# Attention over rows of a 2048-token layer: rotary heads in steps of two query tiles, and the order of TensorE's work in a step

## The reference, cut to what matters

```python
SEQ, CHUNK, HEAD_DIM = 2048, 64, 64
# group A: 8 query heads over 2 key heads, rotary, own chunk + 1 before (A_BAND = 2), a sink per head
sc = einsum('bncvgd,bnlvd->bnvgcl', qc, kb) * HEAD_DIM ** -0.5
m  = max(max(sc, axis=-1), sink);  p = exp(sc - m)
p  = p / (sum(p, axis=-1) + exp(sink - m))
oa = einsum('bnvgcl,bnlvd->bncvgd', p, vb)
# group B: 8 heads, own chunk + 8 before (B_BAND = 9), a clipped relative bias per head
sc = einsum('bnchd,bnlhd->bnhcl', qc, kb) * HEAD_DIM ** -0.5 + bias
ob = einsum('bnhcl,bnlhd->bnchd', softmax(sc), vb)
x  = x + concatenate([rmsnorm(oa), rmsnorm(ob)]) @ w_out
```

## Time and profile before

| what | us |
|---|---|
| median of 3 runs (2800.03 to 2801.11) | 2800.1 |
| the profiled execution, its own time | 2800.31 |
| its span from first to last instruction | 2798.5 |
| attention, from the first scores to the last output | 534.46 to 892.48 |

### The profile page before, as it was taken

One profiled execution on the slowest core, in us unless ns is written; L12 is line 12 of the kernel. 1 busy time (PEld: TensorE's weight loads), 2 busy tenths in 40 slices (PEclk: granted clock), 3 DMA queues, 4 the chain that ended last, 5 costly groups with the idle time before them and its releaser, 6 DMA issues.

```text
span 2798.5 us, 41169 instructions
## 1 busy us (share of the span) xinstructions
PE 2741.3 (98%) x14774; PEld 2249.8 (80%) x14774; DVE 1555.9 (56%) x2465; ACT 1091.2 (39%) x2229; POOL 1087.0 (39%) x882
## 2 busy tenths in 40 slices
PE   9999999999999999999998999999999999999998
PEld 9888888777766788888886888887888887888876
DVE  3356664567676332333336666668766666654364
ACT  6434333377787223333325333334333332222342
POOL 7644454301011112311216555455655453552252
PEclk9999999999999999999999999999999999999999
DMA  8657868534366334022326333335333236544454
GB/s 280 235 179 254 267 210 272 172 125 140 115 184 216 135 132 173 32 89 80 91 64 225 113 98 102 98 99 199 120 110 98 90 110 213 219 145 148 139 171 136
DMA packets 260112, 425.45 MB, mean 152 GB/s; under 512 B 18256, under 2 KB 157520, under 8 KB 258896
## 3 DMA queue, kind: packets, MB, share of 16 engines
q1 hardware_dynamic: 222512, 355.29, 38.5%
q10 hardware_dynamic: 37408, 67.65, 7.8%
HBM read 282.35 MB, written 135.27 MB: 149 GB/s over the span
## 4 chain that ended last, share of the span: by engine, by line
PE 55%; DVE 2%; DMA 1%; POOL 1%; ACT 1%; issue 0%; SPq 0%; POOLq 0%; ACTq 0%; DVEq 0%
PE gu_acc L51 10%; PE gu_acc L52 10%; PE gu_acc L53 10%; PE down_acc L51 4%; PE down_acc L53 4%; PE down_acc L52 4%; PE cross_sum_o L51 2%; PE cross_sum_s L51 2%; PE cross_sum_s L53 2%; PE cross_sum_o L53 2%; PE cross_sum_o L52 2%; PE cross_sum_s L52 2%; PE cross_turned L2185 0%; PE cross_turned L1903 0%; DMA gu_t<-t_d 0%
## 5 line engine op out<-in xcount | busy, mean ns | idle before, releaser
L51 PE MATMUL gu_acc<-gu_t,shared_m 128*128 128x512 f32 x704 | 276.0, 392 | 5.0 <-DVE gu_t L2507 5.0
L52 PE MATMUL gu_acc<-gu_t,shared_m 128*128 128x512 f32 x704 | 275.0, 391 | 0.0
L53 PE MATMUL gu_acc<-gu_t,shared_m 128*128 128x512 f32 x704 | 274.9, 391 | 0.0
L350 POOL TENSOR_TENSOR front_wq_lo<-front_wq_raw,front_wq_hi 128x1024 fp32r<-128x1024 f32 x72 | 178.9, 2486 | 201.9 <-ACT front_wq_hi L346 201.7
L2450 ACT ACTIVATE shared_m<-kept_x 128x512 fp32r<-128x512 f32 x175 | 109.4, 628 | 210.8 <-PE gu_acc L53 187.8
L51 PEld LDWEIGHTS gu_acc<-gu_t,shared_m 128*128 128x128 f32 x704 | 132.8, 189 | 35.6 <-issue 4.7
L53 PEld LDWEIGHTS gu_acc<-gu_t,shared_m 128*128 128x128 f32 x704 | 132.7, 189 | 27.8
L52 PEld LDWEIGHTS gu_acc<-gu_t,shared_m 128*128 128x128 f32 x704 | 132.9, 189 | 27.3
L346 ACT ACTIVATE front_wq_hi<-front_wq_raw 128x1024 fp32r<-128x1024 f32 x72 | 76.2, 1058 | 187.0 <-PE qkv_acc L53 100.7
L51 PE MATMUL gu_acc<-shared_m 128*128 128x512 f32 x352 | 138.0, 392 | 2.9 <-POOL shared_m L2423 2.5
L53 PE MATMUL gu_acc<-shared_m 128*128 128x512 f32 x352 | 137.6, 391 | 0.0
(11 more groups left out here) (353 smaller groups left out, 7653.1 us busy)
## 6 DMA issues: line engine op xcount, KB each, us to landing
front_wq_raw<-in_w_in ACTq DMA_DIRECT2D x69, 512.0 KB, 4.0
head_h<-qk_d SPq DMA_DIRECT2D x48, 512.0 KB, 4.6
ahead_w_even<-in_w_gate SPq DMA_DIRECT2D x44, 512.0 KB, 4.5
kept_x<-in_w_up SPq DMA_DIRECT2D x44, 512.0 KB, 4.3
a_d<-gu_a_mix SPq DMA_DIRECT2D x88, 256.0 KB, 3.2
a_d<-gu_a SPq DMA_DIRECT2D x66, 256.0 KB, 4.2
kept_x<-in_w_down SPq DMA_DIRECT2D x56, 256.0 KB, 4.7
shared_m<-a_d SPq DMA_DIRECT2D x19, 704.0 KB, 4.2
```

The costliest lines, as they stand in the source:

```text
L51: pe.matmul(out, l_hi, r_hi, start=first, stop=False)
L52: pe.matmul(out, l_hi, r_lo, start=False, stop=False)
L53: return pe.matmul(out, l_lo, r_hi, start=False, stop=last)
L350: pool.tensor_tensor(self.lo[:, i % Q_SLOTS, :], self.raw[:, i % Q_SLOTS, :], raw(self.hi[:, i % Q_SLOTS, :]), ALU.subtract).then_inc(self ...
```

## The change

The unit u becomes a step s. In group B a step is one unit, as before; in group A it is two query tiles of a job, so A has 32 steps instead of 64. Scores, exponentials, transposes, values, copies and division of a step of A cover both tiles; the two score tiles stand in the two banks of `sum_s`. TensorE's order in a step is now: scores of t, all transposes of t-2, the output's transpose of t-4, values of t-3. The transposes use three banks: in B head 0's first four tiles, head 1's first four tiles, and the fifth tile of both heads with the output's transpose in the same bank; in A one bank for each of the two query tiles. ScalarE copies the first piece, VectorE the rest; VectorE does the score sums of its step first, then copies, then the division of t-4. Nothing in the SyncE block changes: the quarters, the wait at L1274 and `load` are as they were, and `s_o` still counts two for each unit.

```diff
-    UNITS_ALL = [(J, i) for J in range(len(JOBS)) for i in range(NT)]
-    NB = len(UNITS_ALL)
+    STEPS = ([(J, (i,)) for J in range(N_PAIR) for i in range(NT)]
+             + [(J, (i, i + 1)) for J in range(N_PAIR, 2 * N_PAIR) for i in range(0, NT, 2)])
+    NS = len(STEPS)
...
+    def units(s):
+        return s if s <= A0 else A0 + 2 * (s - A0)
+
+    def job_end(J):
+        return NT * (J + 1) if J < N_PAIR else A0 + NT // 2 * (J + 1 - N_PAIR)
...
+    def pieces(s):
+
+        if is_a(s):
+            return [(j, [(j, x, y) for x in range(2) for y in range(tiles(s, j))]) for j in range(2)]
+        near, last = min(tiles(s, 0), 4), [(0, x, 4) for x in range(2) if tiles(s, 0) > 4]
+        return [(j, part) for j, part in ((0, [(0, 0, y) for y in range(near)]),
+                                          (1, [(0, 1, y) for y in range(near)]), (2, last)) if part]
...
-        turned = [room.bank(f"turned{j}") for j in range(2)]
+        turned = [room.bank(f"turned{j}") for j in range(3)]
         sum_o = room.bank("sum_o")
-        o_turned = room.bank("o_turned")
+        o_turned = turned[2][:, 2 * P:4 * P]
...
-                    act.wait_ge(s_out, NB - (1 - z) * HT)
+                    act.wait_ge(s_out, NS - (1 - z) * HT // 2)
...
-                for step in range(NB + 4):
+                for step in range(NS + 4):
                     if step >= 4:
                         copy_o(step - 4)
-                    if 2 <= step < NB + 2:
-                        copy(act, copied, step - 2, 0, 0)
-                    if 1 <= step < NB + 1:
-                        exp(step - 1, 0)
-                    if 2 <= step < NB + 2:
-                        copy(act, copied, step - 2, 1, 0)
-                    if 1 <= step < NB + 1:
-                        exp(step - 1, 1)
-                    J, late = divmod(step, NT)
-                    if late == 7 and 1 <= J < 2 * N_PAIR:
-                        store(J - 1)
-                    if step == NB - HT + 6:
+                    for lane in range(4):
+                        if 1 <= step < NS + 1 and lane < len(lanes(step - 1)):
+                            exp(step - 1, *lanes(step - 1)[lane])
+                        if 2 <= step < NS + 2 and lane == 0:
+                            copy(act, copied, step - 2, *pieces(step - 2)[0])
+                    for J in range(2 * N_PAIR - 1):
+                        if step == job_end(J) + 5:
+                            store(J)
+                    if step == NS + 1:
                         store_last(0)
...
-                for step in range(NB + 5):
-                    if step >= 5:
-                        divide(step - 5)
-                    if 2 <= step < NB + 2:
-                        copy(dve, dve.tensor_copy, step - 2, 0, 1)
-                    if step < NB:
-                        maxima(step, 0)
-                        maxima(step, 1)
-                    if 2 <= step < NB + 2:
-                        copy(dve, dve.tensor_copy, step - 2, 1, 1)
+                for step in range(NS + 4):
+                    if step < NS:
+                        for lane in lanes(step):
+                            maxima(step, *lane)
+                    if 2 <= step < NS + 2:
+                        for j, part in pieces(step - 2)[1:]:
+                            copy(dve, dve.tensor_copy, step - 2, j, part)
+                    if step >= 4:
+                        divide(step - 4)
...
+                    after(pe, s_max, 2 * units(s))
+                    for j, i in enumerate(tokens):
+                        w, end = width(s, j), (i + 1) * P
+                        halves = [(0, w, j * BANK)] if w <= BANK else [(0, w // 2, 0), (w // 2, w, BANK)]
...
+                    for b, part in pieces(s):
+                        j, x, _ = part[-1]
+                        pe.wait_ge(s_exp, 2 * (units(s) + j) + x + 1)
+                        after(pe, s_copied[b], fillings(s, b))
+                        if b == 2:
+                            after(pe, s_out, s - 2)
+                        for z, (j, x, y) in enumerate(part):
+                            at = columns(s, j, tiles(s, j) * P).start + y * P
+                            last = pe.transpose(turned[b][:, z * P:(z + 1) * P], probs(s, x, slice(at, at + P)),
+                                                ident[:, :])
+                        last.then_inc(s_t[b], 1)
...
+                def turn_out(s):
+                    pe.wait_ge(s_o_sb, s + 1)
+                    after(pe, s_out, s)
+                    after(pe, s_copied[2], fillings(s + 2, 2))
+                    for j in range(len(STEPS[s][1])):
+                        last = pe.transpose(o_turned[:, j * P:(j + 1) * P], o_sb[:, s % 2, j * P:(j + 1) * P],
+                                            ident[:, :])
+                    last.then_inc(s_ot, 1)
+
+                for step in range(NS + 4):
+                    if step < NS:
                         score(step)
-                    if 2 <= step < NB + 2:
-                        turn(step - 2, 1)
+                    if 2 <= step < NS + 2:
+                        turn(step - 2)
                     if step >= 4:
                         turn_out(step - 4)
-                    if 3 <= step < NB + 3:
+                    if 3 <= step < NS + 3:
                         values(step - 3)
```

More of the change, by code:

```diff
@@ L1121, in stage_attention, with is_a, lanes, win @@
     A_FULL = A_WIN * P
[L1123 to L1155, removed]
+    def is_a(s):
+        return s >= A0
+    def units(s):
+        return s if s <= A0 else A0 + 2 * (s - A0)
+    def job_end(J):
+        return NT * (J + 1) if J < N_PAIR else A0 + NT // 2 * (J + 1 - N_PAIR)
+    def lanes(s):
+        return [(j, x) for j in range(len(STEPS[s][1])) for x in range(2)]
+    def win(s):
+        return A_WIN if is_a(s) else B_WIN
+    def tiles(s, j):
+        return min(STEPS[s][1][j] + 1, win(s))
+    def width(s, j):
+        return tiles(s, j) * P - (CHUNK if is_a(s) and tiles(s, j) == win(s) else 0)
+    def columns(s, j, w):
+        full = win(s) * P
+        return slice(j * A_FULL + full - w, j * A_FULL + full)
+    def quarter(s):
+        J, tokens = STEPS[s]
+        return J * N_BLK + tokens[0] // BT
+    def pieces(s):
[4 more added lines that the diff above has]
+                                          (1, [(0, 1, y) for y in range(near)]), (2, last)) if part]
+    uses = [[0] for _ in range(3)]
+    for s in range(NS):
+        for j in range(3):
+            uses[j].append(uses[j][-1] + sum(k == j for k, _ in pieces(s)))
+    def fillings(s, j):
+        return uses[j][min(max(s, 0), NS)]
     LOADS = 4
@@ L1210, in stage_attention, with probs, copy @@
         s_wlo = room.sem("s_w_lo")
[L1212 to L1222, removed]
+        def probs(s, x, at):
+            return (probs_a if is_a(s) else probs_b)[:, s % 2, x, at]
+        def copy(engine, instruction, s, j, part):
+            after(engine, s_o, 2 * units(s - 1) if s >= 1 else 0)
+            engine.wait_ge(s_t[j], fillings(s, j) + 1)
+            if j == 2:
+                after(engine, s_ot, s - 1)
+            heads, n = sorted({x for _, x, _ in part}), len(part) * P
+            unit, _, y = part[0]
+            w = n // len(heads)
+            at = unit * A_FULL + y * P
+            instruction(turned_sb[:, s % 2, heads[0]:heads[-1] + 1, at:at + w],
+                        turned[j][:, 0:n].rearrange("p (h c) -> p h c", h=len(heads))).then_inc(s_copied[j], 1)
         def stored(engine):
@@ L1326, in _, with exp @@
             def _(act):
[L1327 to L1332, removed]
-                        act.wait_ge(s_zero, 4)
[L1334 to L1341, removed]
+                def exp(s, j, x):
+                    act.wait_ge(s_max, 2 * (units(s) + j) + x + 1)
+                    for b in range(3):
+                        after(act, s_t[b], fillings(s - 1, b))
+                    if s in (A0, A0 + 1):
+                        act.wait_ge(s_zero, 4)
+                    after(act, s_out, s - 3)
+                    at, lane = columns(s, j, width(s, j)), 2 * j + x
+                    act.activation(probs(s, x, at), scores[:, s % 2, x, at], ACT.Exp,
+                                   bias=top[:, s % 4, lane:lane + 1], scale=-1.0,
+                                   accum_out=total[:, s % 4, lane:lane + 1]).then_inc(s_exp, 1)
+                    if is_a(s) and lane == 3:
+                        act.wait_ge(s_below, s - A0 + 1)
+                        act.activation(sink_exp[:, s % 4, :], below[:, s % 4, :], ACT.Exp).then_inc(s_sink_exp, 1)
@@ L1415, in maxima @@
                         out=to, in0=from_, in1=add, scale=-0.125, scalar=start, op0=ALU.add, op1=ALU.min,
[L1416 to L1424, removed]
-                    else:
[L1426 to L1429, removed]
+                        accum_out=top[:, s % 4, lane:lane + 1]).then_inc(s_max, 1)
@@ L1462, in score @@
```

(32 more changed lines are left out.)

161 lines of the change are left out of this document (76 added, 85 removed).

## The result

The changed kernel takes 2852.5 us (median of 4 runs, 2848.43 to 2855.41) against 2800.15: ratio 1.0185, 95% interval 1.0168 to 1.0203. The profiled execution took 2853.14 us with a span of 2851.4, 52.9 longer than before.

The account below looks back on a forecast made before the run. TensorE, busy 98% of the span, was taken to bound the kernel. Attention's end at 942.8 instead of 892.5 (+50.3) and the border's +3.7 made +54.0 on 2800.3: 2854 us, range 2822 to 2872.

Parts of the forecast that it names:

- Group B: TensorE's new order in group B: one array-shape change fewer a step, full step 3.67 us, -13 us in all.
- The shape rival: TensorE's 0.17 us gaps belong to semaphore waits, not array-shape changes, so group B gains nothing: 2867 us, chance 0.08.
- The bound of -17 us: Largest gain allowed for group B, if the new order brings no new wait; the other bound was 0.
- Steps of two tiles: Group A's pair step costs TensorE 3.10 us against 3.88, ScalarE and VectorE just hidden; by itself 24 us gained.
- One step in front of a load instead of five: Group A's load release: lead before a quarter's scores falls from 9.7 to 3.1 us, so 14 loads come late.
- the 4.5 and 13 that were named as signs: Expected in group A's profile: 14 TensorE DMA waits of 2 to 4.5 us, loads' first DMAs 10.5 to 13 apart.
- The load: A quarter's load in group A takes 7.5 us from first issue to landing, plus 0.1 to the scores.
- The step that closes the loop: Group A's pair step between a load's landing and the next load's issue: 4.9 us, mostly at half clock.
- Behind the last wait: From the scores of step 94 to attention's last output: 6.2, 1.0 for the clock, 2.2 and 6.1, together 15.5 us.
- The border: Attention to next stage: the norm waits for the last job's store, starting 3.2 us after the last output; +3.7 us.
- with the clock up: Rival: group A's loads come late but TensorE's clock holds at 1.00, steps at 3.25 us: 2832 us, chance 0.22.
- with the loads in time: Rival: group A's loads arrive in time and the change gains, 32 us less: 2768 us, chance 0.10.

Follow-up runs that it names:

- run 1: Changed kernel, but group A's queries and keys load once the score sums allow it, values on their own semaphore; 2764.5 us, ratio 0.9869.
- run 3: Changed kernel with 28 filler transposes of the identity on TensorE ahead of each late load's wait in group A; 2827.3 us, ratio 1.0098.
- run 8: Changed kernel, same load release, but keys and values shared by two group A jobs loaded only for the first; 2806.7 us, ratio 1.0026.
- run 5: Kernel before the change, with group A's loads from the third on released two units later; 2877.3 us, ratio 1.0275.
- run 6: Kernel before the change, late group A loads released two units later, 14 filler transposes of the identity ahead of each wait; 2822.1 us, ratio 1.0077.

## Why the prediction was right

The forecast was 2854 us, the measurement 2852.5. By its own steps:

- *Group B*, -13 us: load 18 went out 13.6 us sooner after attention's start, and the full step is 3.67, as summed. The shape rival is out: the transposes wait for three pieces without a gap. The bound of -17 us was added up wrongly; 10.9 and 5 make 16.
- *Steps of two tiles*, 3.10 us with ScalarE and VectorE hidden: 3.11 in run 1.
- *One step in front of a load instead of five*: 14 waits, as counted, and run 1 shows that they are the cause. They last 3.5 to 4.8 us, with loads 11.4 to 13.8 apart, a little past the 4.5 and 13 that were named as signs.
- *The load*, 7.5 + 0.1 us: measured 7.10 from issue to scores, too long by 0.5. The medians of the earlier trace rows held loads that met the old kernel's stores and the next load; with loads 12.5 us apart the values' DMA lands 5.1 us after its issue in the median, where I had 5.7 on average.
- *The step that closes the loop*, 4.9 us: measured 5.47 from scores to the next load, between 4.6 and 5.9, too short by 0.6. The low clock covered most of these steps whole, and such a step takes 5.9 us, not the 5.6 estimated from the values alone.
- *Behind the last wait*, 15.5 us: measured 17.2 (924.79 to 942.00), too short by 1.7. Its last term, 6.1, was rounded up; its parts add up to 5.9.
- *The border*, +3.7 us: the norm begins 3.35 us behind the last output and began 0.55 before it, 3.9.

So the hit to 2 us is partly luck. Two errors of opposite sign, some 7 us each over 13 quarters, leave 12.51 us a quarter where I had 12.5. Two smaller ones cancel in part: load 18 went out 3.0 us sooner than forecast (754.30 against 757.3), 1.9 of it because attention itself began sooner in this execution, and the end took 1.7 longer. The mechanism does not hang on them. Run 1 took away the late load and gave back 88 us, where the forecast and its rival lie 86 apart. The clock's part was 13 x 1.65 + 1 = 22 us in the sum; run 3 gave 25 and left about 5. Run 8 shortened the load in eight quarters and gave 46 where 38 were expected.

Two of the rivals were priced right and are other kernels: with the clock up 2832, built as run 3, 2827; with the loads in time 2768, built as run 1, 2764.5. The Trainium skill's page "TensorE: Matmul & The Clock Gate", section "HAM oscillation — how this bites in real kernels", has the same picture of half rate behind each DMA wait, and the trace agrees: behind all 14 waits, of 3.5 to 4.8 us, the clock was at 0.50 within 2 us. The shorter waits of run 8, up to 0.9 us, left it at 1.00. The drain at a change of mode, on the Trainium skill's page "TensorEngine Tiling (Array Packing)", section "Tiling Modes", agrees too: the gap, 0.17 us in this case's rows, stands at the changes of shape alone.

## What to carry to other kernels

When steps grow, a release that is counted in the old units comes closer to its use. For each load count the steps between release and use, before and after, and multiply by the step's length: here 9.7 us became 3.1, under a load of 7.1. Release a buffer by its last reader (for queries and keys the scores, as in run 1) rather than by the pipeline's end. Look at the granted clock right behind every wait of TensorE, since it can cost more than the wait: in run 5 two waits of 2.8 us in all stood before a loss of 77.

## What was not expected of the hardware

The half clock can last. In the old order, after one idle time of 1.72 us, it stayed at 1.2 GHz for some 170 us in which TensorE's rows show no idle time (run 5), where filling the wait gave 55 us back (run 6). At attention's start it had come back after 13.6 us. The old kernel never shows this in group A, because nothing there waits. The changed kernel, with 14 waits of about 4 us, lost only about 30 us to the clock. Nor does the length of a wait alone tell whether the clock falls: in run 3 it fell behind a wait of 1.57 us (the one that ended at 832.63) and held behind one of 1.66 (at 896.10). Why is open.
